# Eight throw-away products between the column sums of each passage, and the column step behind both scalings

## The reference, cut to what matters

```python
mod = (c_act @ ada_w[i] + ada_b[i])[:, None, :]
sh_a, sc_a, g_a, sh_f, sc_f, g_f = jnp.split(mod, 6, axis=-1)
h = rms_norm(x, norm_g[i, 0]) * (1.0 + sc_a) + sh_a
y = moba_attention(h, ...)                      # or diff_attention, conformer
x = x + g_a * rms_norm(y, norm_g[i, 1])
h = rms_norm(x, norm_g[i, 2]) * (1.0 + sc_f) + sh_f
x = x + g_f * rms_norm(swiglu(h, ffn_w_in[i], ffn_w_out[i]), norm_g[i, 3])
```

## Time and profile before

| | us |
|---|---|
| median of three runs (1032.02 to 1032.25) | 1032.15 |
| the profiled execution's own time | 1034.28 |
| its span, first to last instruction | 1032.5 |
| PE busy in the span | 976.5 (95%) |
| DVE busy | 845.6 (82%) |
| ACT busy | 543.0 (53%) |
| mean granted TensorE clock | 0.974 |

### The profile page before, as it was taken

One profiled execution on the slowest core, in us unless ns is written; L12 is line 12 of the kernel. 1 busy time (PEld: TensorE's weight loads), 2 busy tenths in 40 slices (PEclk: granted clock), 3 DMA queues, 4 the chain that ended last, 5 costly groups with the idle time before them and its releaser, 6 DMA issues. The chain is left out here.

```text
span 1032.5 us, 19788 instructions
## 1 busy us (share of the span) xinstructions
PE 976.5 (95%) x6740; PEld 893.0 (86%) x6740; DVE 845.6 (82%) x1376; ACT 543.0 (53%) x1013; POOL 54.7 (5%) x102
## 2 busy tenths in 40 slices
PE   3899989999999998998899999999998999999997
PEld 2899978999999887996899999979996689999996
DVE  6779998888888886776888888889998789997775
ACT  2465445444444465565544444449997555555542
POOL 3100002000000011111200000001000000000000
PEclk9999998999999898998999999999998899999999
DMA  9999983999999775561499999984230348966531
GB/s 338 324 330 312 319 280 102 336 311 311 309 310 321 229 211 178 163 204 41 114 342 314 309 312 310 312 267 123 83 123 0 119 141 238 285 190 187 183 123 41
DMA packets 259081, 233.43 MB, mean 226 GB/s; under 512 B 7514, under 2 KB 208987, under 8 KB 259035
## 3 DMA queue, kind: packets, MB, share of 16 engines
q1 hardware_dynamic: 256256, 226.52, 72.3%
q0 software_dynamic: 1536, 4.81, 1.3%
q10 hardware_dynamic: 1242, 1.51, 0.4%
HBM read 231.75 MB, written 1.06 MB: 225 GB/s over the span
## 5 line engine op out<-in xcount | busy, mean ns | idle before, releaser
L1182 DVE TENSOR_TENSOR wlo<-raw,whi 128x1024 fp32r<-128x1024 f32 x286 | 346.9, 1221 | 91.0 <-ACT whi L874 90.5
L488 PE MATMUL work<-h_hi,whi 128*128 128x256 f32 x1440 | 407.8, 283 | 8.8 <-DVE h_lo L1246 7.1
L488 PE MATMUL work<-h_hi,wlo 128*128 128x256 f32 x1440 | 403.1, 280 | 0.0
L488 PE MATMUL work<-h_lo,whi 128*128 128x256 f32 x1440 | 403.0, 280 | 0.0
L874 ACT ACTIVATE whi<-raw 128x1024 fp32r<-128x1024 f32 x286 | 298.2, 1054 | 132.1 <-PE work L488 62.6
L488 PEld LDWEIGHTS work<-h_hi,whi 128*128 128x128 f32 x1440 | 271.6, 189 | 17.3 <-issue 7.2
L488 PEld LDWEIGHTS work<-h_lo,whi 128*128 128x128 f32 x1440 | 271.3, 188 | 3.1
L488 PEld LDWEIGHTS work<-h_hi,wlo 128*128 128x128 f32 x1440 | 271.9, 189 | 0.0
L1194 DVE SCALAR_TENSOR_TENSOR acc<-ada_raw,csil,acc 128x512 f32 (+1 forms) x256 | 191.1, 747 | 4.3 <-DMA ada_raw<-in_ada_w 1.9
L508 PE MATMUL Y<-whi,ab_hi 128*128 128x512 f32 x308 | 99.2, 403 | 0.0
L508 PE MATMUL Y<-whi,ab_lo 128*128 128x512 f32 x308 | 98.0, 399 | 0.0
(11 more groups left out here) (204 smaller groups left out, 1162.2 us busy)
## 6 DMA issues: line engine op xcount, KB each, us to landing
ada_raw<-in_ada_w SPq DMA_DIRECT2D x88, 512.0 KB, 6.6
raw<-in_ffn_w_in SPq DMA_DIRECT2D x88, 512.0 KB, 7.2
ada_raw<-in_mod_w SPq DMA_DIRECT2D x48, 512.0 KB, 6.5
raw<-in_ffn_w_out SPq DMA_DIRECT2D x44, 512.0 KB, 5.2
raw<-in_f_up_w SPq DMA_DIRECT2D x44, 512.0 KB, 4.1
raw<-in_moba_w_qkv SPq DMA_DIRECT2D x24, 512.0 KB, 7.8
raw<-in_diff_w_qkv SPq DMA_DIRECT2D x24, 512.0 KB, 6.1
raw<-in_a_pw_w SPq DMA_DIRECT2D x24, 512.0 KB, 5.5
```

Source lines behind the costliest of these rows:

```text
L488: mm = pe.matmul(dst, w[:, u, ws], h[:, k, :], start=(k == 0 and m == 0), stop=(k == KT - 1 and m == 2))
L1182: dve.tensor_tensor(wlo[:, u, :], raw[:, u, :], whi[:, u, :].bitcast(F32), ALU.subtract).then_inc(lo[u], 1)
```

## The change

`mod_columns` gets a helper that issues one product of 512 columns of `h_hi` into bank 2 of `work`, which nothing reads; it is called ahead of each of the first eight column sums. On DVE the column step moves behind the scaling of both tiles.

```diff
+            def throw_away():
+
+                pe.matmul(work[:, 2, :], h_hi[:, 0, 0:P], h_hi[:, 0:2, :], start=True, stop=True)
+
             def mod_columns(s, layer, b0):
...
                         m, at = (b - b0) * (BLK // P) + n, b * BLK + n * P
+                        if m < 8:
+                            throw_away()
                         mm = pe.matmul(mod_bank[s][:, m:m + 1], acc[:, at:at + P], ones[:, 0:1], start=True, stop=True)
...
                         dve.wait_ge(rsx_done, 2 * s + t + 1)
                         dve.tensor_scalar(xs[:, t, :], xt[:, t, :], rsx[:, t:t + 1], None,
                                           ALU.mult).then_inc(xs_ready, 1)
-                        if t == 0:
-                            columns(s)
-                else:
-                    columns(s)
+                columns(s)
                 dve.wait_ge(mod_cols_used, s + 1)
```

## The result

The changed kernel is slower: 1036.76 us (median of 16 runs, 1031.79 to 1041.37) against 1032.81 us (16 runs, 1030.37 to 1035.79). The ratio is 1.0036, with a 95% interval of 1.0022 to 1.0050, or +3.7 us (+2.3 to +5.2). Forecast were 1033.7 us, +1.6, and a range that ended at 1035.8. The sign of the slip was right, its size less than half. The forecast of 1033.7 was counted from the median of three runs, 1032.15; the sixteen runs have 1032.81, so 0.7 us of its distance from 1036.76 lies in the start of the count and the rest in the slip.

What follows compares the result with a forecast made beforehand. PE was taken to bound the stages, and a scaling, transpose, ACT and DVE chain the passages. Four passages at 0.28 us (1.1) plus 0.5 for the fifth gave +1.6 on 1032.15: 1033.7 us, range 1032.1 to 1035.8.

Steps and rivals of the forecast that it cites:

- What bounds a passage: Each passage's end is set by scaling tile 1, its first transpose, then 5.53 us of ACT and DVE.
- Cost of a throw-away at the high clock: In the column sums on PE: 0.23 us each, eight adding 1.84 us, hidden by the wait for DVE.
- Slip behind the moved column step: Tile 1's first transpose, queued behind tile 0's eighth, comes later: 0.38 us at low clock, 0.17 at high.
- Which clock: Sums' first half and tile 0 at high clock, tile 1 undecided: middle value 0.28 us for each of four passages.
- P + 5.47: Forecast end of the lengthened sums, 5.47 us counted from the start of the column sums in a passage.
- the cover: PE's wait for DVE, hiding longer sums if tile 0 is turned before tile 1 may be; lacking in the fifth passage.
- The sums outgrow their cover: Rival: throw-aways costing up to 0.40 us make PE turn tile 0 late; 1035 to 1038.6 us, chance 0.13.
- The clock is low for tile 1 everywhere: Rival: tile 1's transposes find the low clock in every passage; 2.25 us longer, 1034.4 us, chance 0.13.
- The high clock pays: Rival: tile 1's eight transposes run faster, −2.2 us net, 1029.9 us; chance 0.08 for a gain outweighing the slips.

Runs made afterwards that it cites:

- e3: Changed kernel plus three more 512-column products in the first product of stages 1 to 5, ahead of the waits of k = 2, 4, 6; 1038.57 us.
- e4: Kernel before plus three 512-column products per passage, ahead of the waits of k = 2, 4 and 6; 1033.15 us.
- e2: Kernel before with only the column step moved behind both scalings, no throw-away products; 1035.73 us.
- e5: Changed kernel with the eighth transpose of tile 0 put behind the seventh of tile 1; 1035.67 us.
- e6: Changed kernel with sixteen throw-away products per passage instead of eight; 1040.26 us.
- e8: Kernel before with four throw-aways between the column sums, column step left between the scalings; 1033.66 us.
- e7: Kernel before with four throw-aways behind the column sums, none between them, column step left between the scalings; 1033.89 us, ratio 1.0021.

## Why the prediction was wrong

**What bounds a passage: right.** The chain over the scaling of tile 1, its first transpose and then 5.53 us of ACT and DVE held in all kernels: 5.52 to 5.54 us in every passage, with and without low clock and with three more products (e3, e4).

**Cost of a throw-away at the high clock: right.** 0.23 us forecast; the sums grew by 1.85 us to the start of their last instruction, 1.84 forecast. Two small readings were a little high, without effect: in the row of 3.63 us the instructions of the column sums start 0.109 us apart, not 0.113, and at the high clock transposes do too, not 0.12.

**Slip behind the moved column step: right.** 0.38 us forecast for the low clock, 0.36 measured in the first and third passage, by itself in e2 and taken away in e5. For the high clock 0.17 forecast, 0.11 measured in the fourth passage of the first profile.

**Which clock: the step that failed.** The prediction took "the first half of the sums and tile 0 at the high level" and hence the middle of two values, 0.28 us, for each of the first four passages, and 0.52 for the fifth. The clock did hold through the throw-aways. But it fell in the thin sums behind them in seven of fifteen passages. Then the seven transposes take 1.5 us and not 0.84, the sums up to 0.75 us longer, and tile 0 is still being turned when tile 1 is ready: an amount that the sum had nowhere, since the bounds of the low clock were put on tile 1 alone. By passage, against the mean of three profiles: first and third 0.28 forecast, 0.36 measured; second and fourth 0.28 forecast, 0.78 measured; fifth 0.52 forecast, 1.39 measured. That is 1.6 against 3.7 us.

The numbers for it were on hand: with the sums' end at P + 5.47 and the 0.21 us a transpose of the earlier trace rows, tile 0 is turned at P + 6.96, against 6.48 allowed in the second and fourth passage and 5.96 in the fifth. I had computed the cover only for the case I thought likely. None of the signs that the prediction named for being wrong came up: the 5.5 us held, the first scaled part was later, and a throw-away took 0.23 us. It had no sign for a late tile 0 outside the fifth passage.

**The rivals.** "The sums outgrow their cover" was right as a mechanism and wrong in its condition: it doesn't take a dearer throw-away (it cost 0.23), the low clock in tile 0 is enough. e6, where the cover is gone at the high clock too, and e8, where it lasts, bear it out from both sides. "The clock is low for tile 1 everywhere" held in thirteen of fifteen passages and was priced at 2.25 us; what it left out is the same. "The high clock pays" was wrong, as forecast: e6 keeps the clock up, its 5.52 us don't shrink, and it is slowest. The rule of the Trainium skill, "TensorE: Matmul & The Clock Gate", Part 4, by which transposes don't reach the full rate, doesn't agree with e6: its transposes run 0.11 us apart at a granted clock of 1.00. Tile 1 mostly found the low clock behind thin sums and waits; which of them brought it about no run separates.

## What to carry to other kernels

Work put into an engine's idle time isn't free until the idle time is compared with the work at the engine's slow clock, since the slow clock may be met just there: here tile 0 found it in seven of fifteen passages. Do that sum for every place where the work is repeated, because the shortest cover pays most (1.39 us in the fifth passage, 0.36 in the first and third). Before asking an idle engine to stay warm, ask what the warm clock would shorten on the path: here one transpose, 0.14 us, while the path itself ran over other engines. And when a step is moved on one engine, look at what is queued behind its waiter on the other: eight transposes stood behind one that had to wait, and taking them out of that place gave back 0.36 us wherever they were what came last.

## What the runs showed of the hardware that was not expected

- The point at which the clock falls isn't at a fixed place of the program: in the passage into stage 5 of the kernel before it fell 4.3, 3.3 and 5.5 us after the start of the sums in the three profiles. In the changed kernel this shifts the price of a passage by up to 1.8 us (0.93, 2.75 and 2.40 in the fifth), and the runs of the changed kernel spread over 9.6 us, those before over 5.4.
- The clock fell while PE was busy throughout with column sums of one column each, in e7 and in the second profile of the changed kernel (1.00 up to 832.3, 0.50 from 832.4). A busy PE in the profile was no sign that the clock would hold.
- With sixteen wide products among the sums all five passages repeat to 0.01 us and the clock stays at 1.00 in each. With eight, the fifth passage had 0.93 us where the clock fell behind the transposes, and 2.40 and 2.75 us where it fell inside the sums.
